# Hybrid encoder block: half of the sigmoid gates' projection as seven-product groups between two branches

## The chip, the cores and the metric

The kernel runs on one core of one Trainium2 chip. Its time is the device time of one execution in microseconds (us), smaller is better; the median of three timed runs is given. A core has a matrix engine (TensorE, "PE" in the rows, with "PEld" for its weight loads), VectorE ("DVE"), ScalarE ("ACT"), GpSimd ("POOL") and a queue that issues transfers (SyncE, "SP"). Each engine runs its own list of instructions in order and waits for others through semaphores. All of them share an on-chip memory, SBUF, of 128 partitions; TensorE writes its sums to PSUM, here eight banks of 128 x 512 fp32.

## The reference, cut to what matters

```python
h = rms_norm(x, norm_mix_pre)                    # 512 tokens x 1024
z = h @ w_in                                     # q, k, v, qx, pin and the gates gl
gates = sigmoid(gl).reshape(S, 3, 1024)
ya = window_attention(q, k, v, ...) @ w_branch_a # 16 heads of 64
yx = memory_attention(qx, mk, mv) @ w_branch_x   # 4 heads of 128
yp = (multiscale_pool(pin) * scale) @ w_branch_p
merged = gates[:, 0]*ya + gates[:, 1]*yx + gates[:, 2]*yp
x = x + rms_norm(merged @ w_out, norm_mix_post)
f = silu(h2 @ w_ffn_gate) * (h2 @ w_ffn_up)      # h2 = rms_norm(x), width 2816
x = x + rms_norm(f @ w_ffn_down, norm_ffn_post)
```

All values are fp32. The gates are a 1024 x 3072 projection of the normalised tokens.

## The kernel before

Everything up to the gates is held transposed: 128 output columns on the partitions, 512 tokens along them. A **tile** is 128 output columns by 512 tokens in one PSUM bank. TensorE takes operands in a rounded format (fp32r), so each fp32 operand is split into a rounded part `hi` (one ScalarE copy) and a remainder `lo` (one VectorE subtraction), and each product is three matmuls: hi x hi, hi x lo, lo x hi (`three`, L1658 to L1666). A full tile is 8 blocks of depth times three, 24 matmuls of 512 columns, all recorded at L1664. A "p" or "x" tile has a depth of only 512, so 12 matmuls.

`plan()` writes out the order of the work by hand as **steps**; step s holds one or two tiles. Before the change: eight steps for the memory tokens, k, v, eight of q, four of qx, four of pin (pool inputs), and from step 26 on twelve gate tiles; then, for each pair j of output tiles, two "a" tiles (attention branch) and two steps of a "p" tile and an "x" tile (pool and memory branch), with six further gate tiles after the first and six after the second of these groups. That makes 66 steps. Twelve attention **units** (eight of window attention, four of memory attention) are woven in: unit u has its scores in step 15 + 2u, its softmax after it, its transposes in the middle of the next step's work (`midway`, L1717, after 5/8 of a tile), and its output `unit_out` at the start of step 17 + 2u, in bank 3 (`O_BANK`). The last unit, 11, is transposed in step 38 and put out at the start of step 39. As that bank is taken, tiles rotate over banks 0 to 2 up to step 40 (L290) and over 0 to 3 afterwards; a bank is free when VectorE has taken the tile that was in it.

In each step s ScalarE and VectorE work through a fixed list. ScalarE: copy the unit's output (`o_hi`), `split_hi` of the weights of step s+2, copy the transposed probabilities, and so on; where a step begins a new "a" tile, three sigmoids over 512 columns (L839). VectorE: `o_lo`, `merged_lo`, softmax work, `split_lo` of the weights of step s+2 (L474), and only then the tiles of step s-1: `scaled_take` (a gate tile times the row of 1/rms, L1173) or `merge` (tile times gate, L1260, and a sum onto the merged tile, L1263). `split_hi` of step s+2 waits until TensorE has finished step s-1, whose buffer it reuses. In one step VectorE also copies the row of 1/rms to another place (L1351, at `ROW_MOVES` + 1). SP loads 1 MB of weights for every two steps into one of two raw buffers (`load_chunk`, L564).

The feed-forward part uses **groups of seven block products** (Strassen-Winograd) for its two projections: four tiles (two of `up`, two of `gate`) are a 2 x 2 block problem with weight blocks A11, A12, A21, A22 (512 deep x 256 wide) and token blocks B11, B12, B21, B22 (512 deep x 256 tokens). Weight sums S1 to S4 and token sums T1 to T4 make seven products instead of eight (`products()`, L78; their order on TensorE is P1, P2, P6, P5, P7, P4, P3). One product is 2 x 4 x 3 = 24 matmuls of 256 columns. In the loop (VectorE at L1509, ScalarE at L1034, TensorE at L1900) VectorE does in each group seven `lo` splits (L1423) and four weight sums (L1438) over 1024 columns, four block outs (L1459, 512 columns) and one product over 1024 columns (L1465); ScalarE does seven `hi` copies (L948), three copies of a partial sum (`keep`, L957) and one SiLU over 1024 columns (L962). Token sums are made once.

GpSimd makes the pool windows' sums up to step 29 and small per-row numbers. The names the change uses again are `products`, `SPLIT_ORDER`, `both` and `split_hi`/`split_lo`.

## Time and profile before

| what | value |
|---|---|
| median of 3 runs | 783.38 us (783.29 to 783.66) |
| the profiled execution's own time | 783.49 us |
| its span (first to last instruction) | 781.7 us |
| TensorE busy | 773.8 us (99%), 4454 matmuls |
| VectorE busy | 533.7 us (68%) |
| ScalarE busy | 360.7 us (46%) |
| GpSimd busy | 68.4 us (9%) |
| granted TensorE clock, mean | 0.998 of full speed (2.4 GHz) |
| read from HBM | 83.12 MB, 109 GB/s |

A row of a timeline gives the start in us from the span's start, the length in us, the engine, the line of the kernel, the operation, what it writes <- what it reads, and the number of instructions merged in the row; in brackets stands the idle time before it and what ended that. The length of a matmul contains its way through the pipeline: what TensorE spends on one is the distance to the next start. The same holds, less strongly, on VectorE and ScalarE, where two neighbours overlap by some 0.1 us. The twelve later gate tiles, which the change replaces, stand in steps 42 to 47 and 52 to 57, from 264.25 us on.

### The profile page before, as it was taken

Reading aid. Unit: us, or ns where it says so; the run is one execution under the profiler, and the core shown is the slowest. Engines: PE = TensorE matmul, PEld = TensorE weight load, DVE = VectorE, ACT = ScalarE, POOL = GpSimd, SP = SyncE. Lnnn points to the kernel's source line nnn. Section 1 sums busy time; section 2 is a strip of 40 time slices with the busy share of each in tenths; the row PEclk is TensorE's granted clock in tenths of the full one; section 3 lists DMA queues with packets and bytes.
Section 4 is the critical chain, followed back from the end, with each engine's and each line's share of the span. In section 5 each row is a group of like instructions: output and inputs, shape, how many; then the busy total and the mean of one; then the engine's idle time right before and its main releaser. Section 6 shows DMA issues by size and latency. Waiting matters only on the chain.

```text
span 781.7 us, 11386 instructions
## 1 busy us (share of the span) xinstructions
PE 773.8 (99%) x4454; PEld 672.1 (86%) x4454; DVE 533.7 (68%) x612; ACT 360.7 (46%) x588; POOL 68.4 (9%) x131
## 2 busy tenths in 40 slices
PE   8999999999999999999999999999999999999997
PEld 7888778777877888888888999999999999888885
DVE  6656566676434633635755588888888888999897
ACT  7823445444335223214433564444544445675462
POOL 6110001334000000000001110000011110000002
PEclk9999999999999999999999999999999999999999
DMA  8862213113112233323472013333333346315102
GB/s 303 312 181 78 84 55 108 55 55 108 55 54 80 83 107 108 108 91 126 162 253 68 3 56 109 108 107 107 107 107 107 107 134 215 108 54 165 52 0 108
DMA packets 68069, 85.75 MB, mean 110 GB/s; under 512 B 3504, under 2 KB 57536, under 8 KB 68032
## 3 DMA queue, kind: packets, MB, share of 16 engines
q1 hardware_dynamic: 67568, 84.71, 33.0%
q8 instruction: 25, 0.41, 0.2%
q10 hardware_dynamic: 464, 0.53, 0.2%
q14 instruction: 12, 0.10, 0.0%
HBM read 83.12 MB, written 2.11 MB: 109 GB/s over the span
## 4 chain that ended last, share of the span: by engine, by line
PE 98%; DVE 1%; ACT 0%; POOL 0%; issue 0%; DVEq 0%; POOLq 0%; ACTq 0%
PE pair L1664 91%; PE pair L1793 1%; PE pair L1775 1%; PE pair L1807 1%; PE pair L1782 1%; PE pair L1812 1%; PE pair L1819 1%; PE pair L1743 0%; PE pair L1671 0%; PE pair L1690 0%; DVE wo_lo L474 0%; ACT wo_hi L461 0%; PE pair L1838 0%; PE pair L1855 0%; PE pair L1849 0%
## 5 line engine op out<-in xcount | busy, mean ns | idle before, releaser
L474 DVE TENSOR_TENSOR w_lo<-raw,w_hi 128x1024 fp32r<-128x1024 f32 x64 | 81.8, 1279 | 87.8 <-ACT w_hi L461 87.7
L1664 PE MATMUL pair<-hT_hi,w_hi 128*128 128x512 f32 x336 | 135.4, 403 | 0.0
L1664 PE MATMUL pair<-hT_hi,w_lo 128*128 128x512 f32 x336 | 131.2, 390 | 0.0
L1664 PE MATMUL pair<-hT_lo,w_hi 128*128 128x512 f32 x336 | 130.9, 390 | 0.0
L461 ACT ACTIVATE w_hi<-raw 128x1024 fp32r<-128x1024 f32 x64 | 67.6, 1055 | 99.0 <-PE pair L1664 90.6
L1664 PE MATMUL pair<-T_hi,op_hi 128*128 128x256 f32 x320 | 90.6, 283 | 0.0
L1664 PE MATMUL pair<-T_lo,op_hi 128*128 128x256 f32 x320 | 90.6, 283 | 0.0
L1664 PE MATMUL pair<-T_hi,op_lo 128*128 128x256 f32 x320 | 90.6, 283 | 0.0
L1664 PEld LDWEIGHTS pair<-hT_hi,w_hi 128*128 128x128 f32 x336 | 63.1, 188 | 14.2 <-issue 1.0
L1664 PEld LDWEIGHTS pair<-hT_hi,w_lo 128*128 128x128 f32 x336 | 63.1, 188 | 13.5
L1664 PEld LDWEIGHTS pair<-hT_lo,w_hi 128*128 128x128 f32 x336 | 63.2, 188 | 13.4 <-issue 1.0
L1664 PE MATMUL pair<-B_hi,op_hi 128*128 128x256 f32 x240 | 67.9, 283 | 0.0
L1664 PE MATMUL pair<-B_lo,op_hi 128*128 128x256 f32 x240 | 67.9, 283 | 0.0
L1664 PE MATMUL pair<-B_hi,op_lo 128*128 128x256 f32 x240 | 67.9, 283 | 0.0
L1664 PEld LDWEIGHTS pair<-T_hi,op_hi 128*128 128x128 f32 x320 | 61.4, 192 | 0.0
L1664 PEld LDWEIGHTS pair<-T_lo,op_hi 128*128 128x128 f32 x320 | 61.4, 192 | 0.0
L1664 PEld LDWEIGHTS pair<-T_hi,op_lo 128*128 128x128 f32 x320 | 61.4, 192 | 0.0
L1664 PEld LDWEIGHTS pair<-B_hi,op_hi 128*128 128x128 f32 x240 | 46.1, 192 | 0.0
L1664 PEld LDWEIGHTS pair<-B_lo,op_hi 128*128 128x128 f32 x240 | 46.1, 192 | 0.0
L1664 PEld LDWEIGHTS pair<-B_hi,op_lo 128*128 128x128 f32 x240 | 46.1, 192 | 0.0
L957 ACT ACTIVATE U<-pair 128x512 f32<-128x512 f32 x30 | 17.9, 598 | 57.6 <-PE pair L1664 57.6
L1664 PE MATMUL pair<-bw_hi,ba_hi 128*128 128x512 f32 x112 | 43.6, 389 | 0.0
(233 smaller groups left out, 1668.7 us busy)
## 6 DMA issues: line engine op xcount, KB each, us to landing
raw<-in_w_in SPq DMA_DIRECT2D x42, 512.0 KB, 4.9
raw<-in_w_ffn_up SPq DMA_DIRECT2D x22, 512.0 KB, 4.8
raw<-in_w_ffn_gate SPq DMA_DIRECT2D x22, 512.0 KB, 4.3
W<-in_w_ffn_down SPq DMA_DIRECT2D x8, 1024.0 KB, 5.0
raw<-in_w_branch_a SPq DMA_DIRECT2D x8, 512.0 KB, 4.0
raw<-in_w_out SPq DMA_DIRECT2D x8, 512.0 KB, 3.8
raw<-in_w_ffn_down SPq DMA_DIRECT2D x6, 512.0 KB, 4.9
raw<-in_w_mem_kv SPq DMA_DIRECT2D x4, 512.0 KB, 6.6
```

The source lines that it names most:

```text
L461: eng.activation(hi, src, ACT.Copy).then_inc(weights_hi, 1)
L474: eng.tensor_tensor(lo, raw_view(s), hi.bitcast(F32), ALU.subtract).then_inc(weights_split, 1)
L957: act.activation(kept[u][:, :, :], both("A"), ACT.Copy).then_inc(kept_ready, 1)
L1664: ins = pe.matmul(dst, a, b, start=first and n == 0, stop=last and n == 2, skip_group_check=onto)
L1775: ins = pe.matmul(scores[:, pr // 2, at:at + KEYS], q[lo:lo + 64, 2 * a + pr % 2, ch, :, :].rearrange("p j t -> p (j t)"), k_dup[lo:lo + 6 ...
L1782: ins = pe.matmul(scores[:, i // 2, at:at + N_MEM], qx[:, a, P * i:P * i + P], mk[:, a, :], start=True, stop=True)
L1793: ins = pe.transpose(turned[:, at // 4, P * (at % 4):P * (at % 4) + P], probs[:, i, :], ident[:, :])
L1807: ins = pe.matmul(bk(O_BANK)[64 * half:64 * half + 64, 2 * P * c:2 * P * c + 2 * P], v_c[:, 2 * b + c, 64 * a:64 * a + 64], probs[:, i:i + ...
L1812: ins = pe.matmul(bk(O_BANK), mv[:, m, a, :], probs[:, 4 * m:4 * m + 4, :], start=(m == 0), stop=(m == MT - 1))
L1819: pe.transpose(bk(bank)[:, 0:P], ident[:, :], ident[:, :])
```

## The change

Gate tiles 0 to 11 are still computed as tiles, but are now the four "p" gates 0 to 3 and the eight "x" gates. The other twelve gates (eight of "a", four of "p") are computed as three groups of seven block products (`LATE`), each group four tiles, in the manner of the feed-forward loop, between step 43 and step 44 (`A0`). The plan has 54 steps: up to step 37 the kinds are as before; steps 38 and 39 hold two "p" tiles each, 40 to 43 two "x" tiles each; then come the three groups; then a0 to a3, two steps of two "p" tiles, a4 to a7. Two tiles of 12 matmuls in a step now come from one weight matrix, and merged sums are kept in the gates' own place. GpSimd makes the token sums T1 to T4 from the split token blocks after the last pool map, with eight operations over 1024 columns. Each group's outputs are scaled by the row of 1/rms in two VectorE operations over 1024 columns (`late_scale`). Sigmoids of gates now cover two tiles (1024 columns) each. The weights of steps 44 and up are split only from the last group on. The core of the diff:

```diff
+EARLY_GATES = 12
+LATE = (("a", 0), ("a", 4), ("p", 4))
...
-    def gates(jp):
-        return [[("gate", 6 * jp + 2 * b + i)] for b in range(3) for i in range(2)]
-
-    def merge(jp):
-        a = [[("a", 2 * jp)], [("a", 2 * jp + 1)]]
-        return a + [[("p", j), ("x", j)] for j in (2 * jp, 2 * jp + 1)]
-
-    steps += gates(0) + gates(1)
-    steps += merge(0) + gates(2) + merge(1) + gates(3) + merge(2) + merge(3)
+    def halves(kind, j):
+        return [[(kind, j + i), (kind, j + i + 2)] for i in range(2)]
+    steps += [[("gate", i)] for i in range(EARLY_GATES)]
+    steps += halves("p", 0) + halves("x", 0) + halves("x", 4)
+    steps += [[("a", j)] for j in range(4)] + halves("p", 4) + [[("a", j)] for j in range(4, KT)]
...
+            if kind == "step" and A0 <= n < A0 + 3:
+                eng.wait_ge(late_done, OPS * len(LATE) - 2 + n - A0)
+            elif kind == "step" and n >= 3:
                 eng.wait_ge(tile_full, step_end[n - 3])
             elif kind == "out" and n < 4:
-                eng.wait_ge(tile_full, tile_no[("gate", 23)] + 1)
+                eng.wait_ge(late_done, OPS * len(LATE))
...
-            return at_stream[("step", min(step + 2, NS - 1))] + 1
+            return at_stream[("step", min(step + 2, A0 - 1 if step < A0 else NS - 1))] + 1
...
-        ROW_MOVES, SCALE_BANK = 40, 6
+        ROW_MOVES, SCALE_BANK = 38, 6
...
+            for g in range(len(LATE)):
+                if g == 0:
+                    sp.wait_ge(weights_split, 2 * late_chunk - 2)
+                else:
+                    sp.wait_ge(late_sums, 4 * g)
+                load_late("A11", g)
+                load_late("A12", g)
+                if g == 0:
+                    sp.wait_ge(weights_split, 2 * late_chunk)
+                else:
+                    sp.wait_ge(late_split, late_number(g - 1, 4))
+                load_late("A21", g)
+                if g > 0:
+                    sp.wait_ge(late_split, late_number(g - 1, 5))
+                load_late("A22", g)
+            sp.wait_ge(late_sums, 4 * len(LATE))
+            load_chunk(late_chunk)
+            sp.wait_ge(late_split, late_number(len(LATE) - 1, 5))
...
+            pool.wait_ge(o_full, A_UNITS)
+            pool.wait_ge(tile_full, tile_no[("map", 3)] + 1)
+            def token_block(dst, name):
+                link(pool.tensor_tensor(late_t[dst][0][:, :, :], late_token(name, True).bitcast(F32),
+                                        late_token(name, False).bitcast(F32), ALU.add))
+            def token_diff(dst, a, b):
+                link(pool.tensor_tensor(late_t[dst][0][:, :, :], late_t[a][0][:, :, :], late_t[b][0][:, :, :], ALU.subtract))
+            token_block("T3", "B12")
+            token_block("T1", "B11")
+            token_diff("T1", "T3", "T1")
+            token_block("T2", "B22")
+            token_diff("T3", "T2", "T3")
+            token_diff("T2", "T2", "T1")
+            token_block("T4", "B21")
...
+            def late_operand_hi(g, m):
+                name = products()[m][1]
+                if name[0] == "A":
+                    act.wait_ge(late_in[name], 16 * g + 16)
+                else:
+                    act.wait_ge(late_sums, 4 * g + int(name[1]))
+                if g == 0 and m < 3:
+                    act.wait_ge(tile_full, step_end[A0 - 3 + m])
+                if g == 0 and m == 3:
+                    act.wait_ge(late_t_made, 1)
+                    act.wait_ge(tile_full, tile_no[("gate", EARLY_GATES - 1)] + 1)
+                act.activation(late_op[m % 4][0], late_block(name), ACT.Copy).then_inc(late_hi, 1)
...
+            def late_group(g):
+                late_operand_hi(g, 3)
+                if g:
+                    act.wait_ge(late_done, OPS * g)
+                late_operand_hi(g, 2)
+                act.wait_ge(late_done, OPS * g + 1)
+                if g == 0:
+                    act.wait_ge(late_sums, 1)
+                else:
+                    act.wait_ge(late_blocks, 4 * g - 1)
+                late_keep(g, "U1")
+                late_operand_hi(g, 4)
+                act.wait_ge(late_done, OPS * g + 2)
+                late_operand_hi(g, 5)
+                act.wait_ge(late_done, OPS * g + 3)
+                if g:
+                    act.wait_ge(late_blocks, 4 * g)
+                late_keep(g, "U2")
+                late_operand_hi(g, 6)
+                if g:
+                    late_sigmoids(g - 1, "up")
+                act.wait_ge(late_done, OPS * g + 5)
+                act.wait_ge(late_blocks, 4 * g + 1)
+                late_keep(g, "U3")
+                if g + 1 < len(LATE):
+                    late_operand_hi(g + 1, 0)
+                    act.wait_ge(late_done, OPS * g + 6)
+                    late_operand_hi(g + 1, 1)
+                else:
+                    for i in range(2):
+                        split_hi(act, at_stream[("step", A0 + i)])
+                late_sigmoids(g, "gate")
...
+                if s in (A0 - 6, A0 - 5, A0 - 4):
+                    for i in range(2):
+                        sigmoids(4 * (s - A0 + 6) + 2 * i)
+                if s == A0 - 4:
+                    token_hi("T2")
+                    token_hi("T1")
+                if s == A0 - 3:
+                    token_hi("T3")
+                    token_hi("T4")
+                if s in (A0 - 2, A0 - 1):
+                    late_operand_hi(0, s - A0 + 2)
...
+            def late_block_out(g, name, half, bank, u):
+                dve.tensor_tensor(late_slots(g, name)[:, :, 2 * P * half:2 * P * half + 2 * P], both(bank),
+                                  late_kept[u][:, :, :], ALU.add).then_inc(late_blocks, 1)
+            def late_scale(g, name):
+                dve.wait_ge(late_blocks, 4 * g + (3 if name == "gate" else 4))
+                v = late_slots(g, name)
+                dve.tensor_tensor(v, v, x_rows[1][:, :].unsqueeze(1).to_broadcast([P, 2, SEQ]), ALU.mult)\
+                   .then_inc(late_scaled, 1)
+            def late_finish(g):
+                dve.wait_ge(late_done, OPS * g + OPS)
+                late_block_out(g, "up", 1, "C", "U2")
+                late_scale(g, "up")
...
+            def late_group(g):
+                if g:
+                    late_weight_sum(g, 2)
+                    late_finish(g - 1)
+                late_operand_lo(g, 3)
+                late_operand_lo(g, 2)
+                if g == 0:
+                    token_lo(3, "T3")
+                late_weight_sum(g, 3)
+                late_weight_sum(g, 4)
+                if g == 0:
+                    token_lo(4, "T4")
+                dve.wait_ge(late_done, OPS * g + 2)
+                dve.wait_ge(late_kept_ready, 3 * g + 1)
+                late_block_out(g, "up", 0, "B", "U1")
+                for m in (4, 5, 6):
+                    late_operand_lo(g, m)
+                dve.wait_ge(late_kept_ready, 3 * g + 3)
+                late_block_out(g, "gate", 1, "C", "U3")
+                if g + 1 < len(LATE):
+                    late_operand_lo(g + 1, 0)
+                    dve.wait_ge(late_done, OPS * g + 6)
+                    late_block_out(g, "gate", 0, "D", "U3")
+                    late_scale(g, "gate")
+                    late_weight_sum(g + 1, 1)
+                    late_operand_lo(g + 1, 1)
+                else:
+                    split_lo(dve, at_stream[("step", A0)])
+                    dve.wait_ge(late_done, OPS * g + 6)
+                    late_block_out(g, "gate", 0, "D", "U3")
+                    split_lo(dve, at_stream[("step", A0 + 1)])
+                    late_scale(g, "gate")
+                    late_finish(g)
...
+                if s == A0 - 2:
+                    token_lo(1, "T2")
+                    late_operand_lo(0, 0)
+                if s == A0 - 1:
+                    token_lo(2, "T1")
+                    late_operand_lo(0, 1)
+                    late_weight_sum(0, 1)
+                    late_weight_sum(0, 2)
...
+            def late_product(g, m):
+                name, a, b, bank = products()[m]
+                pe.wait_ge(late_split, late_number(g, m))
+                if g and name == "P1":
+                    pe.wait_ge(late_kept_ready, 3 * g)
+                if g and name == "P2":
+                    pe.wait_ge(late_blocks, 4 * g - 3)
+                if name == "P5":
+                    if g:
+                        pe.wait_ge(late_blocks, 4 * g)
+                    else:
+                        pe.wait_ge(tile_merged, merged_no[tiles[step_end[A0 - 1] - 1]])
+                if name == "P6":
+                    pe.wait_ge(late_kept_ready, 3 * g + 1)
+                if name == "P7":
+                    pe.wait_ge(late_kept_ready, 3 * g + 2)
+                if name == "P3":
+                    pe.wait_ge(late_blocks, 4 * g + 2)
+                if g == 0 and b[0] == "T":
+                    pe.wait_ge(late_t_split, ("T2", "T1", "T3", "T4").index(b) + 1)
+                (whi, wlo), xhi, xlo = late_op[m % 4], late_token(b, True), late_token(b, False)
+                fresh = name not in ("P6", "P7", "P3")
+                for i in range(2):
+                    for k in range(4):
+                        ins = three(both(bank)[:, i, :], whi[:, k, P * i:P * i + P], wlo[:, k, P * i:P * i + P],
+                                    xhi[:, k, :], xlo[:, k, :], fresh and k == 0, k == 3, onto=not fresh)
+                ins.then_inc(late_done, 1)
...
+                if s == A0:
+                    for g in range(len(LATE)):
+                        for m in range(OPS):
+                            late_product(g, m)
+                for n, t in enumerate(steps[s]):
+                    second = steps[s][0][0] == "p"
+                    tile(t, s, midway if n == second else None)
...
```

`late_operand_lo`, `late_weight_sum` and `late_keep` do over `late_op`, `late_sum` and `late_kept` what L1419, L1425 and L955 do in the feed-forward loop; `late_keep` of U1 and U3 share one buffer. `merge` works as before but for the waits and places shown.

## Rows read from the trace of the kernel before

**Rows 1.** The page, part 4: share of the chain that ended last, by engine.

```profile
PE 98%; DVE 1%; ACT 0%; POOL 0%; issue 0%; DVEq 0%; POOLq 0%; ACTq 0%
```

**Rows 2.** The waits of TensorE: who waited <- for whom: us in total, times, longest.

```profile
PE pair L1819 <- POOL ident L696: 2.1, 1, 2.1
```

**Rows 3.** TensorE's timeline: first matmuls of two gate tiles (start us, us, ...).

```profile
269.69 0.39 PE L1664 MATMUL pair<-hT_hi,w_hi 128*128 128x512 f32 x1
...
275.12 0.39 PE L1664 MATMUL pair<-hT_hi,w_hi 128*128 128x512 f32 x1
```

**Rows 4.** TensorE's timeline in the FFN loop: first matmuls of P3 and the next P6.

```profile
482.63 0.28 PE L1664 MATMUL pair<-B_hi,op_hi 128*128 128x256 f32 x1
...
491.27 0.28 PE L1664 MATMUL pair<-T_hi,op_hi 128*128 128x256 f32 x1
```

**Rows 5.** VectorE's timeline in the same loop, from the block out of P4 on.

```profile
482.83 0.69 DVE L1459 TENSOR_TENSOR gate_out<-pair,U 128x512 f32<-128x512 f32 x1
483.44 1.22 DVE L1438 TENSOR_TENSOR sum_odd<-raw 128x1024 f32<-128x1024 f32 x1
...
486.84 0.68 DVE L1459 TENSOR_TENSOR up_out<-pair,U 128x512 f32<-128x512 f32 x1
...
488.58 1.22 DVE L1423 TENSOR_TENSOR op_lo<-sum_even,op_hi 128x1024 fp32r<-128x1024 f32 x1
```

**Rows 6.** ScalarE's timeline in the same loop: an activation over 1024 columns in place.

```profile
483.80 1.04 ACT L962 ACTIVATE gate_out<-gate_out 128x1024 f32<-128x1024 f32 x1
```

**Rows 7.** TensorE's timeline in steps 38 and 39.

```profile
239.82 0.39 PE L1664 MATMUL pair<-oa_hi,w_hi 128*128 128x512 f32 x1
...
246.16 1.88 PE L1812 MATMUL pair<-probs,mv 128*128 128x512 f32 x4
247.47 0.79 PE L1664 MATMUL pair<-oa_hi,w_hi 128*128 128x512 f32 x1
248.10 0.40 PE L1664 MATMUL pair<-oa_lo,w_hi 128*128 128x512 f32 x1
```

**Rows 8.** ScalarE's timeline in steps 38 and 39.

```profile
244.30 1.03 ACT L800 ACTIVATE probs<-pair 128x1024 f32<-128x1024 f32 x1 [3.16 <-PE pair L1793]
245.35 1.28 ACT L839 ACT_TABLE_LOAD   x1
...
248.22 0.58 ACT L822 ACTIVATE ox_hi<-pair 128x512 fp32r<-128x512 f32 x1
248.69 1.05 ACT L461 ACTIVATE w_hi<-raw 128x1024 fp32r<-128x1024 f32 x1
```

**Rows 9.** VectorE's timeline in steps 39, 41 and 44.

```profile
248.83 0.69 DVE L1240 TENSOR_TENSOR ox_lo<-pair,ox_hi 128x512 fp32r<-128x512 f32 x1 [5.82 <-ACT ox_hi L822]
249.77 1.23 DVE L474 TENSOR_TENSOR w_lo<-raw,w_hi 128x1024 fp32r<-128x1024 f32 x1 [0.26 <-ACT w_hi L461]
...
261.31 0.42 DVE L1351 COPY x_row_late<-x_row 128x512 f32<-128x512 f32 x1
...
277.62 0.68 DVE L1173 TENSOR_TENSOR gates<-pair,x_row_late 128x512 f32<-128x512 f32 x1
```

**Rows 10.** TensorE's timeline about a short wait in the output projection.

```profile
400.50 0.50 PE L1664 MATMUL pair<-wo_hi,mrg_hi 128*128 128x512 f32 x1
```

**Rows 11.** VectorE's timeline at that place: what the wait was for.

```profile
399.22 3.50 DVE L474 TENSOR_TENSOR wo_lo<-raw,wo_hi 128x1024 fp32r<-128x1024 f32 x3 [1.28 <-ACT wo_hi L461]
```

**Rows 12.** The page, part 6: issues, KB each, us to landing.

```profile
raw<-in_w_in SPq DMA_DIRECT2D x42, 512.0 KB, 4.9
```

**Rows 13.** Groups of GpSimd's instructions by line: xcount | busy, mean ns | idle before.

```profile
L769 POOL TENSOR_TENSOR S<-f 128x1024 f32<-128x1024 f32 x1 | 2.4, 2402 | 124.2 <-PE pair L1664 124.2
```

**Rows 14.** VectorE's timeline beside GpSimd's sums (165.59) and in step 34 (207.63).

```profile
165.59 2.06 DVE L474 TENSOR_TENSOR w_lo<-raw,w_hi 128x1024 fp32r<-128x1024 f32 x1
...
207.63 1.23 DVE L1235 TENSOR_TENSOR probs<-probs,inv_denom 128x1024 f32<-128x1024 f32 x1
```

**Rows 15.** TensorE's timeline in step 34: the transposes of those probabilities.

```profile
212.68 1.03 PE L1793 MATMUL pair<-ident,probs 128*128 128x128 f32 x8
```

More of the change, by code:

```diff
@@ L831, in take, with sigmoids @@
                     act.activation(op_hi[:, i, :], src, ACT.Copy, scale=scale_p[:, i:i + 1]).then_inc(map_hi_done, 1)
[L833 to L839 removed]
+            def sigmoids(i):
+                act.wait_ge(tile_copied, copied_no[("gate", i + 1)])
+                v = gates[:, i:i + 2, :]
+                act.activation(v, v, ACT.Sigmoid).then_inc(sigmoid_ready, 1)
@@ L1324, in _ @@
                     o_lo(unit_at(s - 2, 0))
-                if s >= 2 and steps[s - 2][0][0] == "p":
+                if s == A0:
+                    for t in steps[A0 - 1]:
+                        merge(t)
+                    for g in range(len(LATE)):
+                        late_group(g)
+                    done += 2
+                if s >= 2 and steps[s - 2][0][0] == "a":
                     merged_lo(steps[s - 2][0][1])
@@ L1831, in _ @@
                 midway = (lambda: unit_turn(unit_at(s, 1))) if unit_at(s, 1) is not None else None
-                for t in steps[s]:
-                    tile(t, s, midway)
-                    midway = None
+                if s == A0:
+                    for g in range(len(LATE)):
+                        for m in range(OPS):
[3 more added lines that the diff above has]
+                    tile(t, s, midway if n == second else None)
                 if s == X_SCALE:
```

160 lines of the change are left out of this document (123 added, 37 removed).

## The prediction

> **What bounds the kernel now.** I began with the chain of waits: 98% of what ended last is TensorE [rows 1]. The list of waits then has a single entry for TensorE, 2.1 us for a constant at the very start [rows 2]. So no engine but TensorE sets the time, and a change can pay only in what TensorE's list contains, less what it makes TensorE wait. Next I read TensorE's own pace, start to start. Two gate tiles of 24 matmuls of 512 columns begin at 269.69 and 275.12: 5.43 us a tile, 0.2265 us a matmul [rows 3]. In the feed-forward loop P3 begins at 482.63 and the P6 three products later at 491.27: 2.88 us a product, 0.120 us for a matmul of 256 columns [rows 4], somewhat more than half of 0.2265. Last I read VectorE and ScalarE where the change gives them another list: the loop [rows 5, 6] and steps 38 and 39 [rows 7 to 9].
>
> **TensorE's work.** Removed are 12 tiles, 12 x 5.43 = 65.2 us. Added are 3 x 7 products, 21 x 2.88 = 60.5 us. That is -4.7 us. The other tiles keep their number of matmuls; they are only reordered. It lies wholly on the path, as TensorE never waits there now.
>
> The Trainium skill, "TensorE: Matmul & The Clock Gate", section "Wait — 56ns, not 53.3ns?", gives a matmul's pitch as its columns over 2.4 GHz plus about 2.5 ns, an estimate of 109 ns for 256 columns and 216 ns for 512. By it the three groups would save some 7 us instead of 4.7. The pitches of this trace, 120 and 226.5 ns, do not agree, and they decide.
>
> **Steps 38 and 39.** The last attention unit ends here, and tiles still rotate over three banks. Step 38 starts at 239.82 [rows 7]. The transposes now come after 18 matmuls instead of 15, so ScalarE's copy of the transposed probabilities, at 244.30 now [rows 8], starts 3 x 0.2265 later, at 244.98, and ends at 246.01: just in time for `unit_out` at 246.16 [rows 7]. Behind it in ScalarE's list stand the table load (1.28 us, [rows 8]) and two sigmoids over 1024 columns. I price these at 1.04 as the SiLU [rows 6], less 0.1 of overlap each: 246.04 + 1.28 + 2 x 0.95 = 249.2. Only then comes `o_hi` of the last unit, which stands at 248.22 now [rows 8]; everything VectorE does in step 39 follows it: `o_lo` 0.61 later, 249.8, `split_lo` another 0.94 later, 250.8 [rows 9], 1.13 on that, 251.9, then the copy of the 1/rms row, which the change moves into just this step (0.42, [rows 9]), then the first `merge`, from 252.4 to 253.05. TensorE's step 39 starts its first short tile at 247.47, as now; its first matmul takes 0.63 [rows 7] and the other 11 about 0.23, so at 250.65 it wants its second tile. That tile goes to bank 2, which held step 38's first tile, and waits for exactly that merge. A wait of TensorE for VectorE ends about 0.05 after the instruction (400.50 behind an end at 399.22 + 3.50 - 2 x 1.13 = 400.46), and its first matmul is 0.11 longer [rows 10, 11]. So the wait costs 253.11 - 250.65 + 0.1 = 2.55 us.
>
> **Step 40.** Its second tile takes bank 1, which held step 39's first tile. VectorE merges that only after `split_lo` of step 42, which follows `split_hi`, which waits for the end of step 39. Now that list reaches the tile of the step before at 277.62, 2.50 after the step's start at 275.12 [rows 3, 9]. With 0.68 for the multiplication and 0.06 the bank is free at +3.24; TensorE wants it after 12 matmuls, at +2.72. Cost 0.52 + 0.1 = 0.6 us. From step 41 on there are four banks, each asked for again two steps later, and the lists fit.
>
> **Into the groups.** In steps 42 and 43 no weights are split; instead VectorE has token remainders, two operand splits and two sums (six operations at 1.13) and the merges. Adding up from the start of step 41 it is some 1.6 us into the first group when the last tile is merged; the remainder of S2 is ready at +3.9 and P6 wants it at 2 x 2.88 = 5.8; that of S3 at +10.3, and P7 wants it at 11.5. Cost 0. The first blocks' transfers are issued at the ends of steps 39 and 41, more than a step ahead.
>
> **Groups two and three.** Here the loop is the measure. VectorE's block out of P4 starts at 482.83 and waits for TensorE, so the list behind it is timed from TensorE; the remainder of S2 ends at 488.58 + 1.22 = 489.80, and P6 starts at 491.27 [rows 4, 5]: 1.47 us in hand. The changed list has two operations more in just this stretch: `late_scale` of the gate half behind that block out, and `late_scale` of the up half behind the block out of P3. Each adds 1.13 of pace, the mean of the three from 483.44 to 486.84 [rows 5], and each waits for the end of the block out right before it, which then takes its length of 0.69 and 0.06 for the wait instead of the 0.61 to the next start [rows 5]. So 2 x (1.13 + 0.14) = 2.54 us more, against 1.47 in hand: 1.07 short, with 0.06 and 0.1 as above 1.2 to 1.25 us for each group that has one ahead of it. Two groups: 2.5 us. The loop's 1024-column product (L1465) comes behind this place and its absence does not help. Behind P6 VectorE waits for TensorE again, so the debt is not handed on. ScalarE's `hi` copy of S2 takes about 1.05 (as in [rows 6]) behind the sum, while VectorE has a block out, a scale and a split to do first (0.75 + 1.13 + 1.13), so it is not late.
>
> **Out of the groups.** Weights of steps 44 and 45 are loaded once S4 of the last group is made (about 2.3 us behind the start of its P6) and split between the last block outs; with 4.9 us for a transfer [rows 12] they are ready some 5 us before the last product ends. The scale and the sigmoids of the last group are needed only by "p" tiles four steps on. The end of the section is as now, with "a" tiles in place of short ones; its chain behind the last tile (multiply, add, `hi`, `lo`) is the same. Cost 0.
>
> **GpSimd's token sums** are eight operations at 2.4 us [rows 13], from about 199 to 220 us, 40 us before they are needed. They cost VectorE: a split beside GpSimd's sums took 2.06 instead of 1.22 [rows 14]. The one place where that could reach TensorE is step 34: the probabilities are scaled by 207.63 + 1.23 = 208.86 and transposed at 212.68 [rows 14, 15], 3.8 us in hand. Two VectorE operations ahead of it, each held up by a whole GpSimd operation, would make 4.8. Bounds 0 and 1.0 us; I take 0, as the measured hold-up is 0.8 and not 2.4.
>
> The Trainium skill, "SBUF — State Buffer", section "Who interferes with whom", says that a VectorE instruction with two SBUF inputs and a GpSimd instruction that reads SBUF take turns, and that the loser waits for the whole instruction. The 2.06 us row agrees in direction. By this rule the upper bound of the sum above holds, and it is rival 3.
>
> **The sum**, on the profiled execution's own 783.49 (span 781.7 and 1.8 around it): 783.49 - 4.7 + 2.55 + 0.6 + 2.5 = 784.4. The median shown is 0.11 below that execution: 784.3 us. The gain in products is there and is given back in waits that the kernel before did not have. For each cost the lower bound is 0 (something I placed ahead of it is quicker); the upper bounds are 3.2 for step 39, if a sigmoid takes as long as the table load (1.28, [rows 8]) instead of 0.95, 1.0 for step 40, if its list is also 0.4 later, and 2 x 2.1 for the groups, if one scale in each, with its repeated row, is as slow as the slowest 1024-column operation shown, 2.06 instead of 1.22 [rows 14].
>
> **Rivals.** 1. The groups do not wait (VectorE is ahead by more than the loop shows): 784.3 - 2.5 = 781.8. For it: the list lacks L1465. Against it: that stands at the wrong place. 2. Steps 39 and 40 do not wait, because the order on ScalarE or the banks are other than I read: 784.3 - 3.15 = 781.15. 3. Slower: GpSimd's sums take turns with VectorE's softmax work in steps 33 to 36, in one unit 1.0 us, in both 2.0: 785.3 to 786.3. It decides once the scaled probabilities are later than 212.68 in step 34. For it: the 2.06 us; against it: the 3.8 us in hand [rows 14, 15]. 4. Neither wait, the whole gain: 784.3 - 5.65 = 778.65.
>
> **How the numbers follow.** A difference of 0.2% (1.57 us: 781.8 to 784.95) is about what can be told from none. Forecast 0.55; rival 1 0.12, which lies on the lower border; rival 2 0.11; rival 3 0.17; rival 4 0.05. Within the forecast its bounds put a tenth above the upper border. Faster 0.05 + 0.11 + 0.06 = 0.22; slower 0.17 + 0.05 = 0.22; same 0.56. The range takes in rivals 1 and 2 and the upper end of rival 3: 781.0 to 786.5; the forecast's own range is 783.0 to 785.5.
>
> **What would show it.** TensorE's waits should list VectorE's merge (the multiplication of L1260) once at 2.5 and once at 0.6 us in steps 39 and 40, and the `lo` split of the late operands twice at about 1.1. The three groups should take 20.2, 21.4 and 21.4 us; `o_hi` of the last unit should start at 249.2. I am wrong if P6 of the second group starts 5.76 us behind its P1, if TensorE's second tile in step 39 starts before 252, or if a wait appears between 200 and 239 us or behind the groups.

## The result, and the profile after

The changed kernel takes 785.73 us, the median of seven executions (783.93 to 786.50), beside 783.38 us for the kernel before in seven executions (782.75 to 783.97). The ratio is 1.0025, with a 95% interval of 1.0016 to 1.0035: 1.3 to 2.7 us slower. The forecast was 784.3.

The seven times fall into two clusters, and most of the step between them goes with the mean TensorE clock that each execution was granted. At 1.000 and 0.999 of full speed they are 783.97 and 783.93. At 0.997 and 0.996 they are 785.65, 785.73, 785.96 and 785.98. One more, at 0.999, took 786.50, which the clock does not explain. The profile shown is of the execution of 785.98, span 784.2, clock 0.997. The mean clock is a coarse sign: in the kernel before the profile has full clock up to 779.0 us and 0.51 behind it, where TensorE has no work left, and that alone makes its mean 0.998; in 38 further executions of it the mean was never lower. A slow stretch of 3.3 us in mid-kernel takes another 0.002. So I read 0.997 or less as a sign of such a stretch; 0.999 or more leaves no room for it, and 0.998 decides nothing.

First the page: part 1's line of busy time (share of the span) and instructions, and part 4's shares of the chain that ended last.

```profile
PE 771.3 (98%) x4670; PEld 679.1 (87%) x4670; DVE 575.6 (73%) x643; ACT 377.6 (48%) x598; POOL 91.0 (12%) x139
...
PE 57%; DVE 1%; issue 0%; ACT 0%; DVEq 0%; POOLq 0%; POOL 0%; ACTq 0%
```

TensorE was busy for 773.8 us before and is for 771.3 now, in a longer span. Against [rows 1], where TensorE had 98% of the chain, it now has 57%: the chain as the page prints it adds up to little more than half of the span, so I read no share of the loss from it, only that it now steps over to VectorE's `late_op_lo` and `late_gates`. The list of TensorE's waits says more (who waited <- for whom: us in total, times, longest):

```profile
PE pair L1945 <- DVE gates L1447: 2.7, 2, 2.4
PE pair L2132 <- POOL ident L784: 2.1, 1, 2.1
PE pair L1945 <- DVE late_op_lo L1466: 1.9, 2, 0.9
PE pair L2027 <- ACT w_hi L1040: 0.5, 1, 0.5
```

[Rows 2] had one entry, the 2.1 us for the constant. The list counts idle time from the end of a matmul's row, which contains its way through the pipeline; what TensorE loses is the distance between two starts less the usual pitch, here some 0.15 us more for each wait. Three entries are new: two waits for VectorE's merge, two for the `lo` split of a late operand, and one of 0.5 us in the first microseconds for the first weights, which differs between executions of one kernel.

**Steps 39 and 40.** TensorE's timeline, which answers to [rows 7]:

```profile
246.38 1.89 PE L2096 MATMUL pair<-probs,mv 128*128 128x512 f32 x4
247.71 0.80 PE L1945 MATMUL pair<-op_hi,w_hi 128*128 128x512 f32 x1
...
250.62 0.39 PE L1945 MATMUL pair<-op_hi,w_lo 128*128 128x512 f32 x1
253.36 0.79 PE L1945 MATMUL pair<-op_hi,w_hi 128*128 128x512 f32 x1 [2.36 <-DVE gates L1447]
...
256.08 0.61 PE L1945 MATMUL pair<-op_hi,w_hi 128*128 128x512 f32 x1
256.51 0.41 PE L1945 MATMUL pair<-op_lo,w_hi 128*128 128x512 f32 x1
...
260.92 0.50 PE L1945 MATMUL pair<-ox_hi,w_hi 128*128 128x512 f32 x1 [0.33 <-DVE gates L1447]
```

The second tile of step 39 starts 2.74 behind the matmul before it, 2.51 more than the pitch of 0.2265. Behind it the pitch is 0.43 (256.08 to 256.51) until it drops back. The tile of step 40 starts 0.72 behind the matmul before it (260.92 against 260.20), so it loses 0.49 (0.33 in the list) and 0.11 for a longer first matmul. The same stretch by windows (us, then busy time with the number of instructions for PE, PEld, DVE, ACT, POOL, then the granted clock, the DMA share and GB/s):

```profile
250.00:253.30 3.30, 1.00 (x5) 0.50 (x3) 2.94 (x5) 2.87 (x4) 0.00 (x0) 0.97 0.00 0
253.30:256.60 3.30, 3.24 (x8) 2.56 (x9) 0.60 (x2) 0.00 (x0) 0.00 (x0) 0.51 0.98 294
256.60:262.00 5.40, 5.07 (x23) 3.84 (x22) 2.43 (x3) 4.05 (x5) 0.00 (x0) 1.00 0.05 16
```

The granted clock is 0.51 for 3.3 us, the lower level (1.2 of 2.4 GHz), directly behind the wait, and 1.00 after it. The seven matmuls from 253.36 on take 3.15 us, up to the start at 256.51, where seven pitches of 0.2265 and the 0.11 for a first matmul would make 1.70. So the stretch cost some 1.45 us in this execution. ScalarE, then VectorE, in the same stretch (compare [rows 8, 9]):

```profile
245.21 1.03 ACT L910 ACTIVATE probs<-pair 128x1024 f32<-128x1024 f32 x1 [3.84 <-PE pair L2077]
246.25 1.28 ACT L947 ACT_TABLE_LOAD   x1
247.54 2.01 ACT L947 ACTIVATE gates<-gates 128x1024 f32<-128x1024 f32 x2
249.46 0.58 ACT L932 ACTIVATE ox_hi<-pair 128x512 fp32r<-128x512 f32 x1
```

```profile
250.07 0.69 DVE L1427 TENSOR_TENSOR ox_lo<-pair,ox_hi 128x512 fp32r<-128x512 f32 x1 [6.84 <-ACT ox_hi L932]
251.02 1.23 DVE L493 TENSOR_TENSOR w_lo<-raw,w_hi 128x1024 fp32r<-128x1024 f32 x1 [0.26 <-ACT w_hi L480]
252.16 0.42 DVE L1624 COPY x_row_late<-x_row 128x512 f32<-128x512 f32 x1
252.61 1.29 DVE L1447 TENSOR_TENSOR gates<-pair,gates 128x512 f32<-128x512 f32 x2
```

VectorE stands idle for 6.84 us, then does three other things before the merge that frees bank 2 at some 253.3.

**The groups.** TensorE: the first product of groups 1, 2 and 3, and the P6 in each. The last row is the tile behind them.

```profile
280.10 0.28 PE L1945 MATMUL pair<-hT_hi,late_op_hi 128*128 128x256 f32 x1
...
300.25 0.28 PE L1945 MATMUL pair<-hT_hi,late_op_hi 128*128 128x256 f32 x1
...
307.11 0.38 PE L1945 MATMUL pair<-late_T_hi,late_op_hi 128*128 128x256 f32 x1 [0.95 <-DVE late_op_lo L1466]
...
321.60 0.28 PE L1945 MATMUL pair<-hT_hi,late_op_hi 128*128 128x256 f32 x1
...
328.46 0.39 PE L1945 MATMUL pair<-late_T_hi,late_op_hi 128*128 128x256 f32 x1 [0.94 <-DVE late_op_lo L1466]
...
342.95 0.40 PE L1945 MATMUL pair<-oa_hi,w_hi 128*128 128x512 f32 x1
```

They take 20.15, 21.35 and 21.35 us. P6 starts 6.86 behind P1 in groups 2 and 3, where two products make 5.76: 1.10 late, and its first matmul is 0.11 longer. VectorE ahead of P6 in group 2 (the splits of the loop's [rows 5], with both scales, L1498, ahead of them):

```profile
...
298.29 1.23 DVE L1498 TENSOR_TENSOR late_gates<-late_gates,x_row_late 128x1024 f32<-128x1024 f32 x1
...
302.84 0.69 DVE L1491 TENSOR_TENSOR late_gates<-pair,late_U 128x512 f32<-128x512 f32 x1
303.56 1.23 DVE L1498 TENSOR_TENSOR late_gates<-late_gates,x_row_late 128x1024 f32<-128x1024 f32 x1
...
305.84 1.22 DVE L1466 TENSOR_TENSOR late_op_lo<-late_sum,late_op_hi 128x1024 fp32r<-128x1024 f32 x1
```

The last one ends at 307.06, and P6 starts at 307.11.

**GpSimd's token sums** run from 194.5 to 217.6 us. A GpSimd row, and what VectorE has in that stretch:

```profile
214.42 3.22 POOL L861 TENSOR_TENSOR late_T<-late_T,late_T 128x1024 f32<-128x1024 f32 x1
```

```profile
205.47 2.15 DVE L1409 TENSOR_SCALAR neg_max<-row_max 128x4 f32<-128x4 f32 x1
...
209.84 2.26 DVE L1422 TENSOR_TENSOR probs<-probs,inv_denom 128x1024 f32<-128x1024 f32 x1
...
212.02 3.40 DVE L493 TENSOR_TENSOR w_lo<-raw,w_hi 128x1024 fp32r<-128x1024 f32 x1
```

VectorE is held up again and again, and TensorE has no wait between 200 and 239 us.

### The profile page after: what moved, and what is told of

It is laid out like the page before. It is cut to its first block, busy times and chain, and to the rows that moved or that the text cites. A ratio compares the mean times of both kernels' runs of the same rounds, so it can differ in the third digit from the quotient of the medians.

```text
span 784.2 us, 11894 instructions
## 1 busy us (share of the span) xinstructions
PE 771.3 (98%) x4670; PEld 679.1 (87%) x4670; DVE 575.6 (73%) x643; ACT 377.6 (48%) x598; POOL 91.0 (12%) x139
## 4 chain that ended last, share of the span: by engine, by line
PE 57%; DVE 1%; issue 0%; ACT 0%; DVEq 0%; POOLq 0%; POOL 0%; ACTq 0%
PE pair L1945 57%; PE pair L1952 0%; DVE late_op_lo L1466 0%; DVE hT_lo L1466 0%; DVE late_sum L1481 0%; DVE x L1672 0%; ACT square L901 0%; DVEq L279 0%; DVE late_gates L1498 0%; DVE late_gates L1491 0%; POOLq L279 0%; POOL meansq L803 0%; DVEq L1933 0%; POOLq L802 0%; ACTq L1306 0%
## 5 line engine op out<-in xcount | busy, mean ns | idle before, releaser
L493 DVE TENSOR_TENSOR w_lo<-raw,w_hi 128x1024 fp32r<-128x1024 f32 x52 | 70.6, 1357 | 44.3 <-ACT w_hi L480 44.3
L1945 PE MATMUL pair<-hT_hi,w_hi 128*128 128x512 f32 x240 | 98.1, 409 | 0.0
L1945 PE MATMUL pair<-hT_hi,w_lo 128*128 128x512 f32 x240 | 93.8, 391 | 0.0
L1945 PE MATMUL pair<-hT_lo,w_hi 128*128 128x512 f32 x240 | 93.6, 390 | 0.0
L480 ACT ACTIVATE w_hi<-raw 128x1024 fp32r<-128x1024 f32 x52 | 54.9, 1055 | 53.5 <-PE pair L1945 40.1
L1945 PEld LDWEIGHTS pair<-hT_hi,w_hi 128*128 128x128 f32 x240 | 45.1, 188 | 10.5 <-issue 1.0
L1945 PEld LDWEIGHTS pair<-hT_hi,w_lo 128*128 128x128 f32 x240 | 45.0, 188 | 9.8
L1945 PEld LDWEIGHTS pair<-hT_lo,w_hi 128*128 128x128 f32 x240 | 45.1, 188 | 9.7 <-issue 1.0
L800 POOL TENSOR_SCALAR meansq<-part_meansq 128x1 f32<-128x1 f32 x16 | 5.5, 343 | 365.7 <-ACT square L901 365.5
```

Of the source, the lines that this page charges most:

```text
L480: eng.activation(hi, src, ACT.Copy).then_inc(weights_hi, 1)
L493: eng.tensor_tensor(lo, raw_view(s), hi.bitcast(F32), ALU.subtract).then_inc(weights_split, 1)
L800: link(pool.tensor_scalar(meansq[:, n:n + 1], part_meansq[:, c:c + 1], 1.0, EPS, ALU.mult, ALU.add))
L1945: ins = pe.matmul(dst, a, b, start=first and n == 0, stop=last and n == 2, skip_group_check=onto)
```

## The experiments

Two theories stood against each other. Theory 1: what is saved in products is given back at three places, each of which waits for VectorE's list (step 39 by its order and by ScalarE's sigmoids, step 40 by a bank, the groups by the scales), and a stretch at half clock comes on top as a consequence of the wait of step 39. Theory 2: the loss lies elsewhere (GpSimd's sums beside VectorE, slower matmuls of the groups, a clock that falls for another reason), and the listed waits only move when they are removed. Each experiment takes one place away, adds one to the kernel before, or combines them. The kernel before, which ran beside them, had a median of 783.73 beside e1 to e4 (17 executions) and 783.34 beside e5 to e8 (21 executions).

### e1: the merge first

```
                     normalise(unit_at(s, 1))
+                if s in (A0 - 5, A0 - 4):
+                    for t in steps[s - 1]:
+                        merge(t)
                 while done < stream_upto(s):
                     split_lo(dve, done)
...
-                if s >= 1 and s != A0:
+                if s >= 1 and s not in (A0, A0 - 5, A0 - 4):
                     for t in steps[s - 1]:
```

> The changed kernel with one edit: in steps 39 and 40 VectorE merges the tiles of the step before ahead of splitting the weights of step s+2 (and ahead of the copy of the 1/rms row). The merge that frees bank 2 then starts 2.6 us earlier in step 39 and the one that frees bank 1 2.4 us earlier in step 40. Theory 1 (TensorE's wait in step 39, 2.5 us, is followed by a stretch at 1.2 GHz which costs some 1.6 to 2 us more, and it is the wait that brings it on): the wait falls to about 0.4, the one of step 40 to 0, no slow stretch, 785.7 - 2.2 - 0.6 - 1.8 = about 781.1. Theory 2 (the slow stretch has another cause, the dense stretch of SBUF traffic or the change's other work): the waits go, 2.8 us, and a stretch at 1.2 GHz stays somewhere from 240 to 265, about 782.9.

Measured: 781.83 us (781.33 to 782.44, 7 executions), ratio to before 0.9970 (0.9959 to 0.9982). Every execution had a clock of 0.998 or 0.999. TensorE's waits:

```profile
PE pair L1948 <- DVE late_op_lo L1466: 1.9, 2, 0.9
PE pair L2030 <- ACT w_hi L1040: 1.4, 1, 1.4
PE pair L1948 <- DVE gates L1447: 0.4, 1, 0.4
```

The waits for the merge shrink from 2.7 in two to 0.4 in one, the groups' 1.9 stays, and with the long wait the slow stretch is gone. It is 3.9 us under the changed kernel's median. By the starts in the two timelines the wait of step 39 costs 1.95 us less (0.57 for 2.51 over the pitch) and that of step 40, 0.6, is gone; the other 1.4 fits the 1.45 of the slow stretch. The 1.4 us at the first weights belongs to the start of this execution (782.44, the slowest of the seven), not to the edit; how much of it the others have, and so how much of the 0.7 by which the median is over 781.1, is not shown.

### e2: the scales later

```
                 late_block_out(g, "up", 1, "C", "U2")
-                late_scale(g, "up")
+                if g + 1 == len(LATE):
+                    late_scale(g, "up")
...
                 late_weight_sum(g, 4)
+                if g:
+                    late_scale(g - 1, "gate")
...
                 for m in (4, 5, 6):
                     late_operand_lo(g, m)
+                if g:
+                    late_scale(g - 1, "up")
...
                     late_block_out(g, "gate", 0, "D", "U3")
-                    late_scale(g, "gate")
```

(and the sigmoids of a group follow on ScalarE in the next group.)

> The changed kernel with one edit: in the second and third group the two scales of the group before are done behind the remainder of S2 (the gate half behind the weight sums, the up half behind the last operand split), and ScalarE's sigmoids follow them. Theory 1 (each group's P6 waits 1.1 us plus a slow first matmul only because two scales stand ahead of that remainder): both waits go, 2.4 us less than the changed kernel, about 783.3, with the wait of step 39 and its slow stretch left. Theory 2 (VectorE has too much work per group as a whole): the wait moves to P7, P4 or P1 of the same group and the time stays within 0.5 us of 785.7.

Measured: 783.47 us (781.58 to 785.59, 11 executions), ratio 0.9991 (0.9980 to 1.0002). The first of TensorE's waits (the others are the constant and 0.9 us for the first weights), and a window of its timeline with the columns as above:

```profile
PE pair L1951 <- DVE gates L1449: 2.6, 2, 2.4
...
```

```profile
255.90:259.40 3.50, 3.50 (x11) 2.67 (x10) 0.00 (x0) 0.00 (x0) 0.00 (x0) 0.54 0.79 269
```

The groups' waits are gone, the 2.6 us of steps 39 and 40 is as it was, and the slow stretch is there with it. Here it does not begin at once: TensorE goes on at 255.02, four pitches are near 0.23, and 0.43 follows from 256.36 on. Six executions with a clock of 0.996 or 0.997 have a median of 783.55, five with 0.998 or 0.999 one of 782.29. So the two places are independent, and the fall of the clock is still there when the groups' waits are gone.

### e3: both, and the first sigmoids one step earlier

The edits of e1 and e2, and the first four gate columns' sigmoids, with the table load, at the end of step 37 instead of in step 38:

```
-                if s in (A0 - 6, A0 - 5, A0 - 4):
+                if s in (A0 - 7, A0 - 5, A0 - 4):
                     for i in range(2):
-                        sigmoids(4 * (s - A0 + 6) + 2 * i)
+                        sigmoids(4 * max(s - A0 + 6, 0) + 2 * i)
```

> The changed kernel with both edits, and the first two sigmoids (with their table load) moved from behind the copy of the transposed probabilities in step 38 to the end of step 37, where ScalarE waits anyway. Theory 1 (three groups of seven products save 4.7 us of TensorE's list and everything else that was lost are four waits and one slow stretch): no wait of TensorE between 200 and 345 us, 783.4 - 4.7 = 778.7, faster by 0.6%. Theory 2 (some of the loss is elsewhere): above 780.

Measured: 778.56 us (778.49 to 778.72, 5 executions), ratio 0.9932 (0.9919 to 0.9946). The chain, TensorE's only wait beside that for the constant (it is for the first weights), and VectorE in step 39:

```profile
PE 98%; DMA 1%; SPq 0%; DVE 0%; ACT 0%; issue 0%; DVEq 0%; POOLq 0%; POOL 0%; ACTq 0%
```

```profile
...
PE pair L1954 <- DVE w_lo L486: 0.4, 1, 0.4
```

```profile
248.70 0.69 DVE L1429 TENSOR_TENSOR ox_lo<-pair,ox_hi 128x512 fp32r<-128x512 f32 x1 [4.64 <-ACT ox_hi L932]
249.30 1.28 DVE L1449 TENSOR_TENSOR gates<-pair,gates 128x512 f32<-128x512 f32 x2
```

The merge begins at 249.30, 3.3 us earlier than in the changed kernel. With every new wait gone, the profiled execution (778.56) is 4.9 us under that of before (783.49); TensorE's start differs little between these two. Beside the 783.73 of the runs next to it the median is 5.2 less (4.2 to 6.3 by the interval). The gain of the products was sized at 4.7. The token sums on GpSimd and the three groups are all still in it, so neither of them carries a loss of its own that would show here: theory 2 falls. It beats both kernels.

### e4: the kernel before, with the wait put in

```
+            pool.wait_ge(tile_full, tile_no[("a", 0)] + 1)
+            for i in range(7):
+                pool.memset(scratch[:, 0:(1024 if i < 6 else 1024)], 0.0).then_inc(held, 1)
+                pool.wait_ge(held, i + 1)
...
             for n in range(NORM_MIX, NORM_POST):
                 inverse_rms(n)
...
                 for k in ks:
+                    if t == ("a", 1) and k == 4:
+                        pe.wait_ge(held, 7)
```

> The kernel before, nothing of the change in it, with an artificial wait of TensorE in step 39: in the middle of tile a1 it waits for seven GpSimd memsets of 1024 columns, started at the end of step 38; by GpSimd's pace for 128 columns (0.2 us) they take 6 to 8 us, so the wait is 2 to 4 us. Theory 1 (a wait of some 2.5 us at this place is enough to bring the clock down): the granted clock is at half speed for about 3.3 us behind it in most executions, and the time is the wait plus 1.6 to 2: 783.4 + 2.5 + 1.8 = about 787.7. Theory 2 (the change's other work is needed for it): clock stays full, 783.4 + wait = about 786.

Measured: 787.89 us (786.30 to 788.19, 5 executions), ratio 1.0047 (1.0034 to 1.0061). The profiled execution took 786.66. TensorE's wait and its timeline there:

```profile
PE pair L1671 <- POOL scratch L758: 2.6, 1, 2.6
```

```profile
250.66 0.39 PE L1671 MATMUL pair<-oa_hi,w_lo 128*128 128x512 f32 x1
253.69 0.50 PE L1671 MATMUL pair<-oa_hi,w_hi 128*128 128x512 f32 x1 [2.65 <-POOL scratch L758]
254.03 0.39 PE L1671 MATMUL pair<-oa_lo,w_hi 128*128 128x512 f32 x1
```

TensorE lost 2.80 us and 0.11. In this execution the pitch behind the wait is back at 0.23 from the second matmul on, and the two executions at a clock of 0.998 took 786.30 and 786.66, about 3.1 us over the kernel before. The other three, at 0.996, took 787.89 to 788.19, 1.6 us more. Nothing of the change is in this kernel, so such a wait is enough to bring the clock down, though not in every execution. No timeline of those three was kept: that their slow stretch stands behind the wait is concluded from the mean clock and from the time, which is lost in about the same amount as in the changed kernel.

### e5: only one scale later

e3, but of the two scales only the up half's is moved (behind the second weight sum of the next group). The debt ahead of P6 is then one scale, 1.27 us against 1.47 in hand.

```
                 late_weight_sum(g, 4)
+                if g:
+                    late_scale(g - 1, "up")
...
                 late_block_out(g, "up", 1, "C", "U2")
-                late_scale(g, "up")
+                if g + 1 == len(LATE):
+                    late_scale(g, "up")
```

> The kernel of e3_all_three, but of the two scales only that of the up half is moved behind the weight sums; the gate half's scale stays where the change put it, ahead of the remainder of S2. Theory 1 (the loop's 1.47 us in hand, less 1.27 for each scale ahead of it): one scale leaves 0.2 us, P6 of groups two and three does not wait, 778.6 as e3_all_three. Theory 2 (the margin was misjudged and the second wait only happened to fit): each P6 waits some 0.3 to 1.2 us, 779.2 to 781.

Measured: 778.62 us (777.99 to 778.75, 5 executions), ratio 0.9936 (0.9923 to 0.9950). TensorE's whole list of waits:

```profile
PE pair L2138 <- POOL ident L784: 2.1, 1, 2.1
```

One scale ahead of P6 costs nothing. The price of the groups is what the two exceed the slack by, not a price for each scale.

### e6: the kernel before, with a shorter wait

e4 with five and a half fills of 1024 columns instead of seven; TensorE waits for the sixth.

```
-            for i in range(7):
-                pool.memset(scratch[:, 0:(1024 if i < 6 else 1024)], 0.0).then_inc(held, 1)
+            for i in range(6):
+                pool.memset(scratch[:, 0:(1024 if i < 5 else 512)], 0.0).then_inc(held, 1)
```

> The kernel before with the artificial wait of e4_before_with_wait at the same place, but shorter: five and a half memsets, about 5.5 us instead of 7.0, so a wait of about 1.3 us instead of 2.8. Theory 1 (it takes a wait of the length of step 39's before the clock falls, as the waits of 1.1 us at P6 were never followed by a slow stretch): full clock in every execution, 783.4 + 1.4 = about 784.8. Theory 2 (any wait at this place does it): in most executions a stretch at half clock, about 786.5.

Measured: 785.38 us (784.37 to 787.26, 11 executions), ratio 1.0024 (1.0015 to 1.0033). The profiled execution is the slowest of them, 787.26. TensorE's waits, and its start and the first of its later matmuls:

```profile
PE pair L1671 <- POOL scratch L758: 1.2, 1, 1.2
PE pair L1752 <- ACT w_hi L873: 1.0, 1, 1.0
```

```profile
7.20 2.04 PE L1752 MATMUL pair<-w_hi,memT_hi 128*128 128x512 f32 x4 [1.04 <-ACT w_hi L873]
...
11.90 0.39 PE L1671 MATMUL pair<-w_hi,memT_hi 128*128 128x512 f32 x1
```

The wait cost 1.38 us and 0.10, and no execution was under 0.998. The rest of this execution's 3.8 us over the profiled one of before is at its start, and not at the wait: the same two matmuls start at 6.06 and 9.62 in the kernel before. So 1.1 us were lost ahead of the first of them and 1.2 between the two, where the pace of 0.43 us a matmul lasts longer. The profile gives a clock of 1.00 there all the same, so the mean clock does not show it. The median is 2.0 over before and 0.6 over what was expected; a start between the two would explain it, but no timeline of the other executions was kept. One other, 787.08, stands as far apart, and four of the 38 executions of the kernel before, at 785.46 to 785.82 with a clock of 0.999, look alike.

### e7: only the sigmoids earlier

The edit shown under e3 alone, on the changed kernel.

> The changed kernel with one edit: the first two sigmoids and their table load stand at the end of step 37 instead of behind the copy of the transposed probabilities in step 38. The last unit's hi copy then starts when TensorE has made it, at about 248.3 instead of 249.4. Theory 1: the wait in step 39 falls from 2.4 to about 1.3, too short for the clock to fall, step 40's wait of 0.4 to 0.5 stays, the two of 1.2 in the groups stay: 785.7 - 1.1 - 1.8 = about 782.8. Theory 2 (the sigmoids are not what the wait hangs on): 785.7 as the changed kernel.

Measured: 782.84 us (782.61 to 783.74, 11 executions), ratio 0.9993 (0.9984 to 1.0002). TensorE's waits (left out are the constant and 1.0 us for the first weights):

```profile
PE pair L1945 <- DVE late_op_lo L1466: 1.9, 2, 0.9
PE pair L1945 <- DVE gates L1447: 1.6, 2, 1.2
...
```

The longest wait for the merge falls from 2.4 to 1.2 (1.39 by the starts instead of 2.51), and the clock stays at 0.998 or above in all eleven. Nearly half of the wait was ScalarE's list; the rest is VectorE's order.

### e8: the merge first and the scales later, sigmoids in their place

> The kernel of e3_all_three without the move of the sigmoids: merges ahead of the weight split in steps 39 and 40, and the scales later. Theory 1: of the four waits one of about 0.4 (plus a slow first matmul) stays in step 39, full clock: 778.6 + 0.5 = about 779.1. Theory 2 (the table load also delays something that the trace does not name): above 780.

The edits of e1 and e2 together. Measured: 779.51 us (779.41 to 779.69, 5 executions), ratio 0.9950 (0.9936 to 0.9963). The wait that is left:

```profile
250.63 0.39 PE L1954 MATMUL pair<-op_hi,w_lo 128*128 128x512 f32 x1
251.43 0.50 PE L1954 MATMUL pair<-op_hi,w_hi 128*128 128x512 f32 x1 [0.41 <-DVE gates L1449]
```

It is 0.95 over e3, though the listed wait is 0.4. By the starts the wait costs 0.57, and the first matmul is 0.11 longer: 0.68. The other 0.25 was there before, as e3 starts the matmul ahead of this place at 250.38 and not at 250.63, and it goes back to the first 13 us. Theory 1 holds, and the table load delays nothing else.

### The clock over all runs

| longest added wait in steps 39 to 40 | kernels | executions with a clock of 0.997 or less |
|---|---|---|
| 2.5 to 2.8 us | changed kernel, e2, e4 | 4 of 7, 6 of 11, 3 of 5 |
| 0 to 1.4 us | e1, e3, e5, e6, e7, e8 | 0 of 44 |
| none | the kernel before, beside them | 0 of 38 |

As a clock of 0.998 does not exclude a slow stretch, the counts of the first line are the least that it can have been.

## Why the prediction was right or wrong

**The products** (-4.7): right. With all new waits removed the profiled execution is 4.9 under that of before (e3); e5, which waits no more than e3, has a median 4.7 under the runs beside it. The products take 2.88 each in the groups too: from P6 of group 1 at 285.85 the next ones follow at 288.73 and 291.61. The 21 of them and the 12 tiles explain it.

**The wait in step 39** (+2.55): right in place, cause and size. ScalarE's probabilities came at 245.21 (predicted 244.98), the two sigmoids took 2.01 (1.90), `ox_hi` came at 249.46 (249.2), the merge began at 252.61 (252.4). Of these distances 0.23 is a later start of this execution (TensorE begins step 39 at 247.71, not at 247.47 as in [rows 7]). TensorE lost 2.51 and 0.11 for a longer first matmul, 2.62. e1 and e7 took away the two halves of the cause one at a time.

**The term that was missing** is what follows that wait. The prediction put the cost of a wait at its length plus 0.1 us, from [rows 10], a wait short enough to leave the clock alone. Behind the 2.5 us wait the granted clock was 0.51 for 3.3 us, which made 1.45 us in the profiled execution; between the two clusters of the executions it is 1.9 us. It accounts for the distance between forecast and median: 783.95 where the clock stayed, against 784.3 forecast, and 785.8 where it fell. For the profiled execution the terms measured add up: -4.9 + 2.62 + 0.6 + 2.4 + 1.45, and 0.23 for its start, make 2.4 of the 2.5 us that it is over the one of before. That no change can be told from none, to which the prediction gave 0.56, holds only for the first kind, and the more frequent kind decided the median. 785.73 lies above the forecast's own range, 783.0 to 785.5. The whole range held it only because it was drawn up to 786.5 for rival 3, whose wait did not come. That was luck, as this cost was not seen.

**The wait in step 40** (+0.6): right in place and size, 0.49 by the starts and a first matmul 0.11 longer.

**The groups** (2 x 1.25): right. P6 was 1.10 + 0.11 late twice, and the groups take 20.15, 21.35 and 21.35 us against 20.2, 21.4 and 21.4. What was read from the loop [rows 4, 5] as 1.47 us in hand is confirmed from both sides: two scales of 2.54 overrun it by 1.1, one of 1.27 stays within it (e5). Taking the two waits away gave 2.3 us by the medians (e8 against e1, which ran at different times) and 2.4 by the timelines, for the 2.5 predicted. That a group hands nothing on to the next is right too, as group 3 loses no more than group 2.

**Out of the groups** (0): right as far as the waits tell, since none is listed there.

**The token sums** (0 within 0 to 1.0): right in the sum, but for too weak a reason, and the cover was nearly used up. GpSimd began at 194.5, not at 199, and in the softmax of step 34 a 128x4 operation took 2.15 instead of 0.17 and the scaling 2.26 instead of 1.23. The probabilities were ready at 212.10, and the transposes began at about 212.9: 0.8 us left of 3.8. The Trainium skill, "SBUF — State Buffer", section "Who interferes with whom", has the two engines take turns by whole instructions; the split of 3.40 beside GpSimd operations of 3.22 agrees: it ends at 215.42, 1.1 behind the end of the GpSimd operation that ran beside it (211.09 + 3.25 = 214.34). The term was put at 0 because the hold-up measured was 0.8 us and not 2.4; here two operations were held up by 2.0 and 1.0, 3.0 together, against 3.8 in hand and 4.8 in the prediction's worst case.

**The rivals.** Rival 1 (the groups do not wait) and rival 2 (steps 39 and 40 do not) are refuted by the list of waits, rival 4 with them; e3 is the kernel that rival 4 described, at 778.56 for its 778.65. Rival 3 gave 785.3 to 786.3, where the time in fact fell, but by a wait of TensorE in steps 33 to 36 that does not exist. Its number was right for a wrong reason.

**Left open:** why the same wait takes the clock down in some executions and not in others (4 of 7, 6 of 11, 3 of 5), the 0.6 us over expectation in e6's median, and single executions such as 786.50 at full clock. For the last two a slow start as in e6's profiled execution is likely, but not shown.

## What to carry to other kernels

Where TensorE is the bound, price a new wait by its cause and then ask how long it is: here waits up to 1.4 us cost their length and 0.1, waits of 2.5 to 2.8 us cost another 1.3 to 1.9 in more than half of the executions (where between 1.4 and 2.5 that begins was not tried). Read a wait's cost from the distance of the starts, since the list of waits gave 0.15 us less each time. Whenever an edit puts work ahead of the instruction that frees an accumulator bank, list what stands in front of it on that engine, and what stands in front of that on the other engine: moving the merges of two steps, the scales of two groups and the first sigmoids, without a single instruction less, turned 2 us lost into 5 us won. Count slack in the unit that consumes it: one scale fitted in the 1.47 us, two did not.

## What the runs showed of the hardware that I had not expected

- TensorE's clock fell from its upper to its lower level (granted 0.51 for 3.3 us) behind a single wait of 2.5 us, though it was busy for 98% of the whole span. In e2 the fall came only 1.2 us after TensorE had gone on. In another kernel it stayed at full speed behind a wait of 2.8 us in the profiled execution, and fell by the mean clock in three of five executions.
- GpSimd's additions over 1024 columns held up even a VectorE operation over four columns (2.15 us for 0.17) and nearly tripled a split (3.40 for 1.23). They were themselves slower beside VectorE, 3.22 us against 2.40 alone [rows 13].
- The profiled executions differ by up to 2.3 us within the first 13 us, by TensorE's wait for the first weights, between 0 and 1.4 us, and by how long the first matmuls keep a pitch of 0.43 instead of 0.23. That is as large as the effects studied here, so their size is read from the timeline and their sign from many executions.
